# Two-block transformer on one core: modulation chunks issued from ScalarE and spread over more stages, 128-row score products first, first weight tiles ahead of tables

## The reference, cut to what matters

```python
# first block, per layer l (c, c_ctx: conditions of 1024 numbers)
shift, scale, gate = split(silu(c) @ w_mod + b_mod, 3)      # the same for c_ctx: 24 rows of 128 outputs each
h = rms_norm(x, norm_g) * (1 + scale) + shift
p = h @ w_in                    # 24 tiles of 128 columns: fourier, pool, q, k, v of 4 heads, gate
s = q @ k.T * 64 ** -0.5        # 4 heads, two maps m of 64 channels each
p = softmax(s[0]) - lam * softmax(s[1]);  o = p @ v
x = x + gate * ((concat(fourier, pool, norm(o)) * silu(g)) @ w_out)

# second block, per layer
sh1, sc1, g1, sh2, sc2, g2 = split(silu(c_2) @ ada_w + ada_b, 6)   # 48 rows of 128 outputs per layer
x = x + g1 * hybrid_mixer(rms_norm(x) * (1 + sc1) + sh1)           # 32 tiles in, 8 tiles out
x = x + g2 * conv_ffn(rms_norm(x) * (1 + sc2) + sh2)               # 44 tiles in (gate, value), 16 out
```

## Time and profile before

| | us |
|---|---|
| median of 3 runs | 2534.73 (2520.99, 2534.73, 2642.1) |
| the profiled execution | 2515.07 |
| its span, first to last instruction | 2513.8 |
| TensorE busy in the span | 2254.3 (90%) |
| mean granted TensorE clock | 0.937 of full |

### The profile page before, as it was taken

How to read it: one execution, slowest core, us unless ns; L and a number is a source line. 1 busy time by engine, 2 the same in 40 slices (tenths; PEclk the granted TensorE clock), 3 DMA queues, 4 the chain that set the end, 5 groups by cost and what they waited for, 6 DMA issues and landing times.

```text
span 2513.8 us, 25927 instructions
## 1 busy us (share of the span) xinstructions
PE 2254.3 (90%) x10488; PEld 1786.8 (71%) x10488; DVE 1285.6 (51%) x1580; ACT 796.4 (32%) x1120; POOL 781.0 (31%) x330
## 2 busy tenths in 40 slices
PE   6799999887999987899988859997899998999998
PEld 2677777774767765788866648775688886878876
DVE  4466657564555655485375441444526346541545
ACT  1345544222444432323323211221222333231321
POOL 0221123222222333322243323432332234444442
PEclk9899999988989898999999879998899998999998
DMA  6322111214322324443224442454131222332332
GB/s 238 121 66 68 52 51 58 64 54 151 92 76 84 93 67 130 153 124 109 68 67 131 130 139 78 142 159 114 54 84 51 59 69 67 95 102 82 99 97 79
DMA packets 313158, 239.83 MB, mean 95 GB/s; under 512 B 6736, under 2 KB 289488, under 8 KB 312400
## 3 DMA queue, kind: packets, MB, share of 16 engines
q1 hardware_dynamic: 313040, 238.17, 31.8%
HBM read 236.05 MB, written 2.10 MB: 95 GB/s over the span
## 4 chain that ended last, share of the span: by engine, by line
PE 73%; DVE 8%; DMA 7%; ACT 5%; issue 4%; POOL 2%; SPq 1%; DVEq 0%; ACTq 0%
PE ps L516 55%; PE ps L1862 2%; PE ps L961 2%; PE ps L958 2%; DMA w_raw_first<-in_w_in 2%; DMA w_raw_second<-in_w_val 2%; POOL w_lo_second L499 2%; PE ps L1582 1%; PE ps L982 1%; ACT a_p L1207 1%; PE ps L851 1%; DMA w_raw_second<-in_w_gate 1%; DVE mod_products_ffn L590 1%; PE ps L993 1%; DMA w_raw_second<-in_w_in 1%
## 5 line engine op out<-in xcount | busy, mean ns | idle before, releaser
L499 POOL TENSOR_TENSOR w_lo_second<-w_raw_second,w_hi_second 128x1024 fp32r<-128x1024 f32 (+1 forms) x200 | 515.0, 2575 | 921.2 <-ACT w_hi_second L493 921.2
L516 PE MATMUL ps<-h_second_hi,w_hi_second 128*128 128x512 f32 x1216 | 504.8, 415 | 85.4 <-POOL w_lo_second L499 62.9
L516 PE MATMUL ps<-h_second_lo,w_hi_second 128*128 128x512 f32 x1216 | 486.1, 400 | 0.0
L516 PE MATMUL ps<-h_second_hi,w_lo_second 128*128 128x512 f32 x1216 | 485.7, 399 | 0.0
L493 ACT ACTIVATE w_hi_second<-w_raw_second 128x1024 fp32r<-128x1024 f32 (+1 forms) x200 | 221.5, 1108 | 526.0 <-PE ps L516 355.2
L516 PEld LDWEIGHTS ps<-h_second_hi,w_hi_second 128*128 128x128 f32 x1216 | 236.1, 194 | 160.3 <-POOL w_lo_second L499 74.1
L499 POOL TENSOR_TENSOR w_lo_first<-w_raw_first,w_hi_first 128x1024 fp32r<-128x1024 f32 x64 | 159.9, 2498 | 467.6 <-ACT w_hi_first L493 467.0
L516 PE MATMUL ps<-h_hi,w_hi_first 128*128 128x512 f32 (+1 forms) x640 | 259.3, 405 | 35.4 <-POOL w_lo_first L499 22.7
L516 PEld LDWEIGHTS ps<-h_second_hi,w_lo_second 128*128 128x128 f32 x1216 | 235.7, 194 | 51.7
L516 PEld LDWEIGHTS ps<-h_second_lo,w_hi_second 128*128 128x128 f32 x1216 | 237.0, 195 | 47.7 <-issue 1.9
L516 PE MATMUL ps<-h_hi,w_lo_first 128*128 128x512 f32 (+1 forms) x640 | 233.7, 365 | 0.0
(11 more groups left out here) (265 smaller groups left out, 3475.8 us busy)
## 6 DMA issues: line engine op xcount, KB each, us to landing
w_raw_second<-in_w_in SPq DMA_DIRECT2D x64, 512.0 KB, 4.2
w_raw_first<-in_w_in SPq DMA_DIRECT2D x48, 512.0 KB, 5.1
w_raw_second<-in_w_gate SPq DMA_DIRECT2D x44, 512.0 KB, 4.1
w_raw_second<-in_w_val SPq DMA_DIRECT2D x44, 512.0 KB, 4.0
w_raw_second<-in_w_down SPq DMA_DIRECT2D x32, 704.0 KB, 4.9
mod_w_ffn<-in_ada_w_turned SPq DMA_DIRECT2D x43, 512.0 KB, 3.7
mod_w_in<-in_w_mod_turned SPq DMA_DIRECT2D x28, 512.0 KB, 3.7
mod_w_mixer<-in_ada_w_turned SPq DMA_DIRECT2D x24, 512.0 KB, 3.9
```

The lines of the kernel that those rows point to most:

```text
L499: k.nc.gpsimd.tensor_tensor(lo, raw, hi.bitcast(F32), ALU.subtract).then_inc(k.sem.weight_split, 1)
L516: last = tensor.matmul(k.ps[:, bank, 0:count], w[:, cut], x[q][:, first:first + count], start=(q == 0 and n == 0), stop=(q == t.k - 1 and ...
```

## The change

The chunk loads move from SyncE's list into ScalarE's: `load_chunks(k, stage, i)` is called one tile ahead, at the end of tile i - 1 (in ("in", l): at step 4i + 1; in ("out", l): before the rounding of tile i + 1), with the same wait for the buffer. The sums stay on VectorE beside tile i. The conditions of the second block are loaded from ScalarE too. The plan is spread: ("in", 1) has 20 chunks (30 before), ("out", 0) and ("out", 1) theirs one tile later (up to tile 7), ("in2", 0) and ("in2", 1) 24 each (24 and none), four of them beside tile 3; ("ffn", 0, 0) 9, ("ffn", 0, 1) 12, ("ffn", 1, 0) 8 (21, 22 and none). The first three tiles of ("in", l) load ahead of the tables, the first two of layer 0 behind the last chunk of `w_mod_first`. The scores form three 128-row products, then the four 64-row products, then the last 128-row product.

```diff
@@ plan_chunks
-            beside(stage, i, place, ..., (3, 3, 4, 5)[place],
+            beside(stage, i, place, ..., 3 if place < 2 else 2 + place + 2 * stage[1],
...
-            first(*((("in", 0), i + 1) if i < 20 else (("out", 0), i - 20)), l, c, (0, 1))
+            first(*((("in", 0), i + 1) if i < 20 else (("out", 0), i - 19)), l, c, (0, 1))
...
-            if i % 2:
-                second(("in", 1), i)
-        for i in range(7):
+        for i in range(1, 8):
             second(("out", 1), i)
-        for i in range(24):
-            second(("in2", 0), max(i, 2))
-        for half in (0, 1):
-            for i in range(3, 22):
-                second(("ffn", 0, half), i)
-                if i >= 19 + half:
-                    second(("ffn", 0, half), i)
+        for l in (0, 1):
+            for i in range(24):
+                second(("in2", l), max(i, 3))
+            for half in (0, 1):
+                for i in sorted([*range(4, 22, 2), *((5, 9, 13) if l == 0 and half else ())]):
+                    if n < (96 if l else 64):
+                        second(("ffn", l, half), i)
@@ linear_sync, linear_scalar, load_chunks
-        for c in k.chunks.get((stage, i), ()):
-            load_chunk(k, c)
...
+        if conditions and i == 3:
+            silu_conditions(k, *conditions, (0,))
         if evacuate:
             evacuate(u)
+        if conditions and i == 1:
+            k.nc.scalar.wait_ge(k.sem.weight_used, own[0] + 1)
+            scalar_load_condition(k, conditions[0], 0, 2)
+        load_chunks(k, stage, i + 1)
+def load_chunks(k, stage, i):
+    for c in k.chunks.get((stage, i), ()):
+        if c.free:
+            k.nc.scalar.wait_ge(k.sem.mod_done, c.free)
+        k.nc.scalar.dma_start(k.mod_places[c.place][1][c.buffer][:, :], c.source).then_inc(c.landed[0], 16)
@@ score_tensor
-    for m, bank, column, b, w in SCORE_PIECES[j >= TX // P]:
...
+    for piece in pieces:
+        high(piece, True)
+    for i, piece in enumerate(reversed(pieces)):
+        done = low(piece, False)
+        if i == 0:
+            done.then_inc(n.scored_third, 1)
+            k.score_thirds += 1
+    tensor.wait_ge(n.scored_third, k.score_thirds)
+    low(last, True)
+    high(last, False).then_inc(n.scored, 1)
@@ first_scalar
+        if s % 4 == 1:
+            load_chunks(k, ("in", l), i)
@@ first_out_scalar
-    for u in own[1:] if l == 0 else own[1:-1]:
-        round_tile(k, u + 1)
+    for i, u in enumerate(own):
+        load_chunks(k, ("out", l), i)
+        if i and (l == 0 or i < KT - 1):
+            round_tile(k, u + 1)
@@ start_sync
     load_first_chunk(k, MOD_SLOTS)
+    for u in (0, 1):
+        load_tile(k, u)
@@ first_sync
-        load_tile(k, u)
-        if i == 1:
+        if l or i > 1:
+            load_tile(k, u)
+        if i == 2:
             sync.wait_ge(s.weight_used, own[0] + 1)
@@ mixer_scalar
+        if i == 0:
+            scalar_load_condition(k, 2, 0, 2)
+        if i == 2:
+            silu_conditions(k, 2, 3 + 2 * l, (0,))
+        load_chunks(k, ("in2", l), i + 1)
```

More of the change, by code:

```diff
@@ L445, in second @@
             place = ("in", "out", "in2", "ffn").index(stage[0])
-            beside(stage, i, place, self.dram["ada_w_turned"][n // 48, n % 48 * P:(n % 48 + 1) * P, :], (3, 3, 4, 5)[place],
+            beside(stage, i, place, self.dram["ada_w_turned"][n // 48, n % 48 * P:(n % 48 + 1) * P, :],
+                   3 if place < 2 else 2 + place + 2 * stage[1],
                    [((1, 1, 0, 0)[place], self.mod2[:, n:n + 1], self.column("ada_b_2", n))])
@@ L526, in multiply_tile, with linear_sync @@
         multiply_rows(k, u, p, range(k.tiles[u].k), ready, after)
[L529 to L532 removed]
+def linear_sync(k, stage):
+    for u in k.stage_tiles[stage]:
         load_tile(k, u)
[L534 to L538 removed]
 def linear_gpsimd(k, stage, then):
@@ L567, in linear_vector, with sum_chunks @@
             evacuate(u)
-        for c in k.chunks.get((stage, i), ()):
-            sum_chunk(k, c)
-def load_chunk(k, c):
-    sync = k.nc.sync
-    if c.free:
-        sync.wait_ge(k.sem.mod_done, c.free)
-    sync.dma_start(k.mod_places[c.place][1][c.buffer][:, :], c.source).then_inc(c.landed[0], 16)
+        sum_chunks(k, stage, i)
+def load_chunks(k, stage, i):
[3 more added lines that the diff above has]
+        k.nc.scalar.dma_start(k.mod_places[c.place][1][c.buffer][:, :], c.source).then_inc(c.landed[0], 16)
+def sum_chunks(k, stage, i):
+    for c in k.chunks.get((stage, i), ()):
+        sum_chunk(k, c)
 def sum_chunk(k, c):
@@ L596, in load_condition, with scalar_load_condition @@
     k.nc.sync.dma_start(k.mod_places[place][0][:, v, :], k.dram["conditions"][which:which + 1, :].broadcast_to(
+        [P, D])).then_inc(k.sem.condition_landed, 16)
+def scalar_load_condition(k, place, v, which, done=0):
+    if done:
+        k.nc.scalar.wait_ge(k.sem.mod_done, done)
+    k.nc.scalar.dma_start(k.mod_places[place][0][:, v, :], k.dram["conditions"][which:which + 1, :].broadcast_to(
         [P, D])).then_inc(k.sem.condition_landed, 16)
@@ L1740, in layer_vectors @@
     s, vector = k.sem, k.nc.vector
-    vector.wait_ge(s.mod_done, k.chunks_done[((("out", 1), ("in2", 0)), (("ffn", 0, 1), ("ffn", 0, 1)))[l][j]])
+    vector.wait_ge(s.mod_done, k.chunks_done[((("out", 1), ("in2", 0)), (("ffn", 0, 1), ("in2", 1)))[l][j]])
     vector.scalar_tensor_tensor(k.gains2[:, 8 * j:8 * j + 8], k.modulation(l, (SC1, SC2)[j], 8), 1.0,
@@ L2118, in mixer_vector @@
                 rest_of_head(k, l, n)
-        for c in k.chunks.get((("in2", l), i), ()):
-            sum_chunk(k, c)
+        sum_chunks(k, ("in2", l), i)
     gate_head(k, l, 3)
@@ L2371, in scalar_program @@
         for half in (0, 1):
-            linear_scalar(k, ("ffn", l, half), True, ffn_scalar(k, l, half), (3, 4, (0,)) if l == half == 0 else None)
+            linear_scalar(k, ("ffn", l, half), True, ffn_scalar(k, l, half), None if half else (3, 4 + 2 * l))
             linear_scalar(k, ("down", l, half), half == 0)
@@ L2397, in sync_program @@
         first_sync(k, l)
-        first_out_sync(k, l)
+        linear_sync(k, ("out", l))
     second_start_sync(k)
     for l in range(2):
-        linear_sync(k, ("in2", l), 2 if l == 0 else None)
+        linear_sync(k, ("in2", l))
         linear_sync(k, ("out2", l))
         for half in (0, 1):
-            linear_sync(k, ("ffn", l, half), 3 if l == half == 0 else None)
+            linear_sync(k, ("ffn", l, half))
             linear_sync(k, ("down", l, half))
```

59 lines of the change are left out of this document (19 added, 40 removed).

## The result

The kernel after takes 2367.39 us (median of 4, 2363.13 to 2371.58), the one before 2527.86 (median of 4): ratio 0.9385, 95% interval 0.9328 to 0.9442. The profiled execution took 2363.13 us, its span fell from 2513.8 to 2361.8, by 152.0 us where the sum had 112.3.

A forecast was written before the change was run, and what follows sets the result against it. TensorE, busy 90% of the span, bounds the kernel; only its waits, low clock and excess work can be won. Terms sum to -112.3 from 2515.1, so 2403, forecast as 2408 us for unprofiled runs; range 2375 to 2455.

The forecast's parts named there:

- feed-forward, layer 0: Second block's feed-forward, layer 0: stall behind chunk loads in SyncE's list goes; -87 us, from -91 to -70.
- ("ffn", 1, 0): Layer 1's first feed-forward half: its 8 new chunks cost +1 us, bounds 0 to 8.
- mixers: ("in2", 0) and ("in2", 1): stall stays in layer 0, is new in layer 1; +13 us, bounds 0 and +25.
- start of the second block: Tables and first weight tile wait for a later chunk sum, which nothing hides; +3.7 us, bounds 0 to 5.
- first tiles: ("in", l): tile 2 no longer lands behind the tables, and the first tile starts earlier; -19 us, -24 to -8.
- scores: Score blocks of 8 products: six fewer row-mode changes, 37.4 us, three quarters counted; -28 us, bounds 0 and 48.
- ScalarE waiting, ten sums fewer: First block: ScalarE's chunk loads wait for sums, ("in", 1) has 10 sums fewer; +4 us, bounds -5 and +20.
- a rival of 158 us: Attention stage: ScalarE's waits hold evacuations (130) and the 28 us of score gain are lost; 2566 us, chance 0.03.
- Rival A: Score steps: VectorE and ScalarE pace them, or changing halves costs too; 14 to 28 us less gain, 2430 us, chance 0.18.
- Rival B: Score blocks: 64-row products in different halves overlap, 11 us more, all 37 realised; about 2385 us, chance 0.10.
- the stall ahead of tile 4 of ("in2", l): Mixers: four chunk loads on ScalarE precede tile 4's rounding, two waiting for sums; TensorE gap of 9 us.
- rival C: Second block: chunk and weight transfers collide, weight tiles land 3 us late or more; +38, 2445 us, chance 0.09.

The follow-up runs named there:

- old order in after: The kernel after with the score products in the order of the kernel before: 2406.27 us, ratio to before 0.9559.
- ten sums more in after: The kernel after with 30 chunks in ("in", 1), ten fewer in ("in2", 1) and ("ffn", 1, 0), still issued from ScalarE: 2376.10 us.
- the dense run: The kernel after with one chunk beside every tile 3 to 21 in layer 0's feed-forward halves, 15 in ("in2", 1), ScalarE issuing: 2361.17 us.

## Why the prediction was off

Point by point, in its own terms (span before less span after, 152.0 us):

| term | forecast | measured | by |
|---|---|---|---|
| feed-forward, layer 0 | -87 | -85.5 | stages |
| ("ffn", 1, 0) | +1 | -1.6 | stages |
| mixers | +13 | +5.7 | stages |
| start of the second block | +3.7 | +3.6 | stages |
| first tiles | -19 | -15.2 (2.2, 5.8, 7.2) | stages |
| scores | -28 | -39 | old order in after |
| ScalarE waiting, ten sums fewer | +4 | -13 (-9 to -13) | ten sums more in after |
| ("out", l) | 0 | -0.9 | stages |
| not in the sum (norms, down, rest of the first block) | 0 | -6 | remainder |

*Right.* The stall of the feed-forward stages and its size, read from the kernel's own control layer; that the term came out within 2 us is partly luck, as two errors in it offset each other (below). The start of the second block: the tables went out at 901.45, behind a sum that began at 900.07 on VectorE, and TensorE stood 12.1 us for the roots. The mode changes: (2.94 - 1.74) / 6 is 0.20 us each, 0.195 in the forecast.

*Wrong, the term "ScalarE waiting in the first block".* This is the step that failed, by 13 to 17 us. It saw the ten sums that leave ("in", 1), and put them at the end of a bound, as -5. They are worth 9 to 13. VectorE was busy 135 of 242 us there, and I took an engine with over a third of its time free as one that holds nobody up. The attention chain runs through it in turns with ScalarE; that a sum of 1.3 to 3 us in its in-order list delays the turn is the likely way, argued from the waits above. The wait of ScalarE for sums, which I priced at +4 with a rival of 158 us behind it, is small in ("in", l) of after (7.6 us in four waits, the longest 4.0 where I had 8.1 at most), and SyncE issuing the same plan gives the stage no shorter. It would have counted with 30 chunks in the stage.

*Wrong, the term "scores".* Three quarters of 37.4 were taken on the ground that the others would pace TensorE. In layer 0 its waits did grow, from 15.6 to 19.2 us; but the clock gave that back (0.96 to 0.97, 1% of 258 us), and the sum held no clock for this stage. Rival A fell. Rival B's 2385 (2388 by its own terms: 2403 - 9 - 11 + 5) was the nearest number, for a wrong reason: halves do not overlap, a block takes 1.74 us in either order where B wanted 1.42. Its other half, all of the 37, was right.

*Mis-sized, the stall ahead of tile 4 of ("in2", l)*: 5.94 and 6.62 us, forecast 9. The place and the maker were right; the working laid the silu (2.3) ahead of the chunk's landing. (Its terms also add up to 13.7 to 14.1 us and not to the 13.5 that it went on with.) ScalarE's timeline at that place in after:

```profile
943.20 0.82 ACTq L576 DMA_DIRECT2D mod_w_mixer<-in_ada_w_turned  x2
943.68 0.59 ACT L2000 ACTIVATE g_key<-ps 128x512 f32<-128x512 f32 x1
944.29 1.28 ACT L613 ACT_TABLE_LOAD   x1
945.59 1.06 ACT L613 ACTIVATE conditions_mixer<-conditions_mixer 128x1024 f32<-128x1024 f32 x1
949.10 1.80 ACTq L576 DMA_DIRECT2D mod_w_mixer<-in_ada_w_turned  x2
951.00 1.06 ACT L492 ACTIVATE w_hi_second<-w_raw_second 128x1024 fp32r<-128x1024 f32 x1 [4.36 <-DVE mod L592]
```

The first two loads stand behind the silu in the list and go out at 943.20, before it and even beside the evacuation. The transfer runs beside the silu, and that silu is most of the 3 us that the forecast has too much. The Trainium skill has the rule (Perfetto Trace Analysis, DVE / Act Engine Instruction): the sequencer hands an operation to a queue and goes on to the next. A load with nothing to wait for thus leaves as soon as it is reached.

*Mis-sized inside the feed-forward term:* the 58.7 and the 32.7 hold some 9.9 us each of a late last activation (11.9 and 11.7 us before, 2.0 in layer 1). After keeps 3.7 of each, because its last sum stands beside tile 20, as the run without it shows. Without it the halves are at 132.0 and 121.9 us, just layer 1's: the other chunks, 9 and 12 and even 19 and 19, cost nothing where I took 4 us. So the sum kept 4 us for a cost that was not there, and gave up 7.4 that stayed.

*First tiles*, -15.2 for -19: the gaps ahead of tile 2 are gone in both layers and the one at the first product with the tables in layer 1 is 2.61 us where I had about 3, but the starts of the stages are only 5.8 and 7.2 us shorter where I had 8 and 9. Where the rest stays is open. The 2.2 us of the first tile are 3 to 6 in the other runs with after's start.

*Transfers from two queues* (rival C) did not collide: the dense run moved 176 GB/s through a feed-forward half with TensorE at 119.87 us busy of 125.63. The Trainium skill's rule that a DMA engine takes turns between queues (DMA: Bandwidth & Descriptors, Queues, rings and completion order) bears on layer 1: there the chunk left ScalarE's queue at 548.2 and took 9.3 us, the last table left SyncE's at 547.3 and took 13.2, so the later one landed first, at 557.5 against 560.5. The trace agrees with the rule. No run shows what it gained.

## What to carry to other kernels

Before pricing moved background work, add up what leaves a stage as carefully as what enters it; an engine idle for a third of a stage can still stand in the bound's chain, and there each of its operations may have a price (here about 1 us for a chunk and its sum). If a load waits for a buffer, count the distance to its release: at one chunk in two tiles either list did; at one per tile it has to stand where its wait is over when the list reaches it, as in the dense run, where ScalarE never waited for a sum in a feed-forward half. Group products by the number of rows they use, and put no side work beside the last tile ahead of a stage that needs its output.

## What the runs showed of the hardware

In the score blocks a change between 128 and 64 rows costs 0.20 us, a change between the halves nothing. A VectorE sum that takes 1.28 us alone took 4.17 when GpSimd's split ran beside it, and the cast behind it 3.31. From the timeline of after, at the end of ("ffn", 0, 0):

```profile
1369.39 3.22 POOL L498 TENSOR_TENSOR w_lo_second<-w_raw_second,w_hi_second 128x1408 fp32r<-128x1408 f32 x1 [3.97 <-ACT w_hi_second L492]
1369.52 4.17 DVE L592 CUSTOM_DVE_ANT_0 mod_products_ffn<-mod_w_ffn,conditions_ffn,cols 128x1024 bf16<-128x1024 f32 x1
...
1374.21 3.15 POOL L498 TENSOR_TENSOR w_lo_second<-w_raw_second,w_hi_second 128x1408 fp32r<-128x1408 f32 x1 [1.61 <-ACT w_hi_second L492]
1374.33 3.31 DVE L2278 CAST act_hi<-act_value 128x512 fp32r<-128x512 f32 x1
1377.67 0.69 DVE L2279 TENSOR_TENSOR act_lo<-act_value,act_hi 128x512 fp32r<-128x512 f32 x1
1378.42 0.29 PEld L515 LDWEIGHTS ps<-act_hi,w_hi_second 128*128 128x128 f32 x1 [6.18 <-DVE act_lo L2279]
```

The split ends at 1372.61, the sum 1.1 us later, about its own 1.28; the next split ends at 1377.36 and the cast 0.3 us later. Both look as if they had waited for GpSimd and then run. It is the same wherever a sum is long: all 41 sums of after over 1.6 us started while a GpSimd operation ran, and ended 1.08 to 1.09 us after it. The cast took 0.43 us in the other 42 of its 44 places, and in all 44 with no chunk beside tile 20. The Trainium skill has this as an exclusive lock (SBUF — State Buffer, SBUF: two separate sides): VectorE and GpSimd share one pair of ports, and whoever comes first keeps it to its end, GpSimd's operation or one of VectorE's that has two SBUF inputs or runs in a two-port mode. For the sum, which has two, the trace agrees; in which mode the cast ran no row tells. I had priced sums at 1.3 to 1.5 us wherever they lie.
